# Per-head RMS means from split squares, and normed queries and keys placed by transfers, in a hybrid decoder layer

## The reference, cut to what matters

```python
def rmsnorm(x, g):
    x32 = x.astype(jnp.float32)
    y = x32 * lax.rsqrt(jnp.mean(x32 * x32, axis=-1, keepdims=True) + NORM_EPS)
    return (y * g.astype(jnp.float32)).astype(x.dtype)

q = rmsnorm(split_heads(q, NSA_HEADS), q_g)            # and the same for ks, kw, fox_q, fox_k
```

```python
a = jnp.exp(log_a)
b = jnp.sqrt(-jnp.expm1(2.0 * log_a)) * (i * xc).astype(jnp.float32)
_, h = lax.associative_scan(linear_combine, (a, b), axis=1)
return h.astype(u.dtype) * jax.nn.silu(z)
```

## Time and profile before

| what | value |
|---|---|
| median of 3 timed runs | 424.03 us (423.52 to 424.44) |
| the profiled execution | 423.8 us, its span 422.0 us |
| TensorE busy | 413.8 us, 98% of the span |
| VectorE busy | 286.5 us, 68% |
| ScalarE busy | 260.2 us, 62% |
| granted TensorE clock | 1.00 throughout |

### The profile page before, as it was taken

How to read it: one execution, slowest core, us unless ns; L and a number is a source line. 1 busy time by engine, 2 the same in 40 slices (tenths; PEclk the granted TensorE clock), 3 DMA queues, 4 the chain that set the end, 5 groups by cost and what they waited for, 6 DMA issues and landing times.

```text
span 422.0 us, 6560 instructions
## 1 busy us (share of the span) xinstructions
PE 413.8 (98%) x2234; PEld 325.8 (77%) x2234; DVE 286.5 (68%) x615; ACT 260.2 (62%) x516; POOL 65.6 (16%) x124
## 2 busy tenths in 40 slices
PE   8999999999999899999999999999899999999996
PEld 6876788879888766666677987988676688888885
DVE  3767749988998966776368756699877389422205
ACT  4846996687565887886087778771888554322200
POOL 5100000000000657565000000000466100000000
PEclk9999999999999999999999999999999999999999
DMA  7922534421213000000321323437610115721005
GB/s 265 355 82 96 161 95 125 120 73 45 101 50 102 0 1 2 2 1 2 119 90 66 101 75 119 132 96 181 189 42 2 50 57 208 279 96 61 2 0 199
DMA packets 13297, 40.51 MB, mean 96 GB/s; under 512 B 1848, under 2 KB 2104, under 8 KB 13008
## 3 DMA queue, kind: packets, MB, share of 16 engines
q1 hardware_dynamic: 13264, 40.09, 29.6%
HBM read 32.17 MB, written 2.10 MB: 81 GB/s over the span
## 4 chain that ended last, share of the span: by engine, by line
PE 84%; DVE 10%; issue 2%; ACT 1%; POOL 1%; POOLq 0%; DVEq 0%; ACTq 0%
PE bank L1417 12%; PE bank L1419 11%; PE bank L1418 11%; PE bank L1599 6%; PE bank L1580 6%; PE bank L1689 5%; PE bank L1688 5%; PE bank L1690 5%; PE bank L1570 4%; PE bank L1571 3%; PE bank L1489 2%; PE bank L1621 2%; PE bank L1390 2%; PE bank L1392 2%; PE bank L1391 2%
## 5 line engine op out<-in xcount | busy, mean ns | idle before, releaser
L1417 PE MATMUL bank<-xh,wh 128*128 128x512 f32 x240 | 99.7, 415 | 0.0
L1419 PE MATMUL bank<-xh,wl 128*128 128x512 f32 x240 | 93.8, 391 | 0.0
L1418 PE MATMUL bank<-xl,wh 128*128 128x512 f32 x240 | 93.8, 391 | 0.0
L997 DVE TENSOR_TENSOR wl<-raw,wh 128x1024 fp32r<-128x1024 f32 (+1 forms) x51 | 61.3, 1205 | 35.6 <-ACT wh L614 35.3
L614 ACT ACTIVATE wh<-raw 128x1024 fp32r<-128x1024 f32 (+1 forms) x51 | 52.6, 1038 | 30.9 <-PE bank L1690 28.4
L1417 PEld LDWEIGHTS bank<-xh,wh 128*128 128x128 f32 x240 | 45.1, 188 | 14.8 <-issue 5.4
L1221 DVE CUSTOM_DVE_ANT_0 bank<-bank,mask_row 128x256 f32<-128x256 f32 (+3 forms) x96 | 46.6, 499 | 13.1 <-PE bank L1571 12.8
L1418 PEld LDWEIGHTS bank<-xl,wh 128*128 128x128 f32 x240 | 45.2, 188 | 11.2 <-issue 2.6
L1419 PEld LDWEIGHTS bank<-xh,wl 128*128 128x128 f32 x240 | 45.1, 188 | 9.7
L591 POOL TENSOR_SCALAR probs<-probs,rcp,gates 128x384 f32<-128x384 f32 (+3 forms) x44 | 26.5, 613 | 136.3 <-DVE rcp L1241 136.2
L1688 PE MATMUL bank<-wh,yh 128*128 128x512 f32 x96 | 37.4, 389 | 0.0
(11 more groups left out here) (243 smaller groups left out, 769.7 us busy)
## 6 DMA issues: line engine op xcount, KB each, us to landing
raw<-in_w_in SPq DMA_DIRECT2D x36, 512.0 KB, 3.4
raw<-in_w_out SPq DMA_DIRECT2D x12, 512.0 KB, 3.3
x_raw<-in_xT SPq DMA_DIRECT2D x4, 512.0 KB, 7.5
x_res<-in_x_tok SPq DMA_DIRECT2D x1, 2048.0 KB, 9.6
out_y<-y_out SPq DMA_DIRECT2D x8, 256.0 KB, 2.2
raw<-in_w_in SPq DMA_DIRECT2D x3, 384.0 KB, 3.1
cmp_w_sb<-in_cmp_w SPq DMA_DIRECT2D x1, 1024.0 KB, 6.8
kh_fox<-kh_fox SPq DMA_DIRECT2D x8, 128.0 KB, 2.3
```

The source lines that it names most:

```text
L997: dve.tensor_tensor(wl[:, c % HL, cols], raw[:, c % RAW, cols], wh[:, c % HL, cols].bitcast(F32), ALU.subtract).then_inc(wl_ready, 1)
L1417: pe.matmul(dst, hi, xh[:, k, :], start=(k == 0), stop=False)
L1418: pe.matmul(dst, hi, xl[:, k, :], start=False, stop=False)
L1419: mm = pe.matmul(dst, lo, xh[:, k, :], start=False, stop=(k == KT - 1))
```

## The change

What it does, for each normed chunk:

- ScalarE also rounds the square to a high part, and VectorE writes the low part of the square (`square_low`). The mean is then two fp32r products with the rounded matrix `block_r`, accumulated in one bank; it stands ahead of block k = 7. Two banks alternate.
- The seeds lose the Identity; VectorE computes the Newton step from the mean in the bank, with constants folded into the gains (two small instructions at the start of the program).
- High and low parts of the normed chunk are each written whole (128 partitions) to one buffer `parts`, and four SP transfers per chunk bring them to their places. The next chunk's high part waits for all of them.
- ScalarE's square now stands ahead of the weight split.
- The recurrence tail of block 2 moves from nq 2 and vn 0 to fq 0 and fq 1 on VectorE, its output product from zl 3 to fq 2. Within a tail the order of instructions is as it was. Buffers are laid out anew for it.

The diff, cut to its core:

```diff
-TAIL_AT = (AT["ks", 0], AT["kw", 0], AT["nq", 0], AT["nq", 1], AT["nq", 2], AT["vn", 0], AT["vf", 2], AT["vf", 2])
+TAIL_AT = (AT["ks", 0], AT["kw", 0], AT["nq", 0], AT["nq", 1], AT["fq", 0], AT["fq", 1], AT["vf", 2], AT["vf", 2])
 OUT_ORDER = (2, 1, 0, 3)
...
         fg = v_nsa[:, :, VN_W - FG_W:]
+        with ExitStack() as w:
+            parts_nsa = sb("parts_nsa", [P, 4, SEQ], F32R, w)
         o_nsa = sb("o_nsa", [P, HEADS // 2, SEQ])
+        block_r = sb("block_r", [P, P], F32R)
         k_cmp_parts = sb("k_cmp_parts", [P, KVH, 2, CMP_PAD], F32R)
...
                     probs = sb("probs", [P, P_RING - 2, SEQ], F32, w)
+                    with ExitStack() as p:
+                        parts_fox = sb("parts_fox", [P, 4, SEQ], F32R, p)
                     pT = sb("pT", [P, 2, 2, PT_W], F32, w)
...
                 q_fox = sb("q_fox", [P, HEADS, SEQ], F32R, m)
-                kh_fox = sb("kh_fox", [P, HEADS, SEQ], F32R, m)
-                kl_fox = sb("kl_fox", [P, HEADS, SEQ], F32R, m)
+                k_fox = sb("k_fox", [P, HEADS, 2, SEQ], F32R, m)
                 q_first = sb("q_first", [P, 2, SEQ], F32R, m)
...
+        def norm_bank(n):
+            return (NORM_W if n % 2 else MEAN)[:, :]
         def nth_normed(c):
...
-            return sum({"nq": 0, "fq": 0, "fk": 2}.get(CHUNKS[x][0], 4) for x in NORMED[:c])
+            return 4 * c
+        def norm_parts(c):
+            return parts_nsa if nth_normed(c) < NSA_NORMED else parts_fox
...
-                n = nth_normed(c)
-                sp.wait_ge(h_ready, 2 * n + 2)
-                sp.wait_ge(l_ready, n + 1)
+                kind, j = CHUNKS[c]
+                sp.wait_ge(l_ready, nth_normed(c) + 1)
+                if nth_normed(c) == NSA_NORMED:
+                    sp.wait_ge(s_ready, NSA_UNITS)
+                parts = norm_parts(c)
                 for s in range(2):
                     own, other = half_of(s), half_of(1 - s)
-                    planes = key_planes(c, s)
-                    for plane in planes[:1] if CHUNKS[c][0] == "fk" else planes:
-                        sp.dma_start(plane[other, :].bitcast(F32), plane[own, :].bitcast(F32)).then_inc(stacked, 16)
+                    if kind in ("nq", "fq"):
+                        q = (q_nsa if kind == "nq" else q_fox)[:, 2 * j + s, :]
+                        copies = ((q[own, :], parts[own, 2, :]), (q[other, :], parts[own, 3, :]))
+                    elif kind == "fk":
+                        k = k_fox[:, 2 * j + s, :, :]
+                        copies = ((k[own, :, :], parts[own, 2:4, :]), (k[other, 0, :], parts[own, 2, :]))
+                    else:
+                        k = k_nsa[:, s + (KVH if kind == "kw" else 0), :, :]
+                        copies = ((k[own, :, :], parts[own, 2:4, :]), (k[other, :, :], parts[own, 2:4, :]))
+                    for dst, src in copies:
+                        sp.dma_start(dst.bitcast(F32), src.bitcast(F32)).then_inc(stacked, 16)
...
-                sp.wait_ge(h_ready, 2 * nth_normed(AT["fq", i]) + 2)
                 if i == 0:
+                    sp.wait_ge(stacked, 16 * stack_copies(nth_normed(AT["fq", 1]) + 1))
                     sp.wait_ge(cmp_prod, 2)
-                elif i in Q_SLOT:
+                else:
+                    sp.wait_ge(stacked, 16 * stack_copies(len(NORMED)))
+                if i in Q_SLOT:
                     sp.wait_ge(fox_consts, 4)
                     sp.wait_ge(proj_done, proj_units(Q_SLOT[i] - HL + 1))
-                else:
+                elif i > 0:
                     sp.wait_ge(s_ready, NSA_UNITS + PAIR_UNITS)
...
                 k = c - STACK_LAG
-                if 0 <= k < N_IN and CHUNKS[k][0] in ("ks", "kw", "fk"):
+                if k == AT["fq", 2]:
+                    place_queries(0)
+                if k in NORMED:
                     stack(k)
-                if k == AT["fq", 0]:
-                    place_queries(0)
                 if k == AT["vf", 3]:
...
                     act.activation(sq[:, :], qr[:, n % 2, :], ACT.Square).then_inc(sq_ready, 1)
+                    act.wait_ge(sq_ready, n + 1)
+                    act.activation(norm_parts(c)[:, 0, :], sq[:, :], ACT.Copy).then_inc(sq_high, 1)
...
                         act.wait_ge(normed, n)
-                    rsqrt_seed(MEAN[:, :], 64.0 if eighth else 1.0, std[:, :], work[:, :],
-                               NORM_W[:, :]).then_inc(norm_seed, 1)
+                    link(act.activation(std[:, :], norm_bank(n), ACT.Ln, bias=eps64 if eighth else eps1,
+                                        scale=64.0 if eighth else 1.0))
+                    link(act.activation(std[:, :], std[:, :], ACT.Exp, scale=-0.5))
+                    act.activation(work[:, :], std[:, :], ACT.Square).then_inc(norm_seed, 1)
...
                     act.wait_ge(normed, n + 1)
-                    if kind == "fq" and j == 0:
-                        act.wait_ge(s_ready, NSA_UNITS)
-                    for s in range(2):
-                        high, _ = operand_parts(c, s)
-                        act.activation(high, qr[half_of(s), n % 2, :], ACT.Copy).then_inc(h_ready, 1)
+                    if n >= 1:
+                        act.wait_ge(stacked, 16 * stack_copies(n))
+                    act.activation(norm_parts(c)[:, 2, :], qr[:, n % 2, :], ACT.Copy).then_inc(h_ready, 1)
...
                     dve.wait_ge(norm_seed, n + 1)
-                    link(dve.tensor_tensor(work[:, :], work[:, :], NORM_W[:, :], ALU.mult))
-                    link(dve.scalar_tensor_tensor(std[:, :], work[:, :], 1.5, std[:, :], ALU.add, ALU.mult))
+                    scale = 64.0 if kind in ("nq", "fq") else 1.0
+                    link(dve.scalar_tensor_tensor(work[:, :], norm_bank(n), EPS, work[:, :], ALU.add, ALU.mult))
+                    link(dve.scalar_tensor_tensor(std[:, :], work[:, :], -3.0 / scale, std[:, :], ALU.add, ALU.mult))
                     dve.scalar_tensor_tensor(qr[:, n % 2, :], qr[:, n % 2, :], ch(GAIN[kind]), std[:, :], ALU.mult,
...
                     n = nth_normed(c)
-                    for s in range(2):
-                        high, low = operand_parts(c, s)
-                        dve.wait_ge(h_ready, 2 * n + s + 1)
-                        ins = dve.tensor_tensor(low, qr[half_of(s), n % 2, :], high.bitcast(F32), ALU.subtract)
-                    ins.then_inc(l_ready, 1)
+                    parts = norm_parts(c)
+                    dve.wait_ge(h_ready, n + 1)
+                    dve.tensor_tensor(parts[:, 3, :], qr[:, n % 2, :], parts[:, 2, :].bitcast(F32),
+                                      ALU.subtract).then_inc(l_ready, 1)
+            def square_low(c):
+                if c in NORMED:
+                    parts = norm_parts(c)
+                    dve.wait_ge(sq_high, nth_normed(c) + 1)
+                    dve.tensor_tensor(parts[:, 1, :], sq[:, :], parts[:, 0, :].bitcast(F32),
+                                      ALU.subtract).then_inc(sq_low, 1)
...
                     zl_gate(2)
-                    lru_output(2)
                 evac(AT["zl", t])
...
                         gates_of(2)
-                    if k == KT // 2 + 1 and c - 1 in NORMED:
+                    if k == KT - 1 and c - 1 in NORMED:
                         head_mean(c - 1)
...
                 n = nth_normed(c)
-                pe.wait_ge(sq_ready, n + 1)
-                if n >= 1:
-                    pe.wait_ge(norm_seed, n)
-                pe.matmul(MEAN[:, :], block_mean, sq[:, :], start=True, stop=True).then_inc(norm_mean, 1)
+                pe.wait_ge(sq_low, n + 1)
+                if n >= 2:
+                    pe.wait_ge(normed, n - 1)
+                parts = norm_parts(c)
+                pe.matmul(norm_bank(n), block_r[:, :], parts[:, 0, :], start=True, stop=False)
+                pe.matmul(norm_bank(n), block_r[:, :], parts[:, 1, :], start=False, stop=True).then_inc(norm_mean, 1)
...
                     continue
+                if c in NORMED:
+                    before(c)
                 split_ahead(c)
                 if c == AT["u", 2]:
                     lru_sigmoids(0)
-                before(c)
+                if c not in NORMED:
+                    before(c)
...
                 norm(c - 1)
+                square_low(c)
                 low_parts(c - 1)
...
                 lru_tails(c)
+                if c == AT["fq", 2]:
+                    lru_output(2)
```

51 lines of the change are left out of this document (22 added, 29 removed).

## The result

The changed kernel takes 427.62 us (median of 4 runs, 426.90 to 429.23) beside 424.01 for the kernel before on the same chip (4 runs). The ratio is 1.0098, interval [1.0085, 1.0111]: one per cent slower, outside the forecast range. The four runs stand apart by TensorE's granted clock: 426.90 and 427.01 at a mean of 1.0, 428.22 at 0.996, 429.23 at 0.992. So 427.0 is the time at full clock, 3.0 us above the kernel before, and 0.7 of the 3.6 goes with the clock. The profiled one is the 426.90, span 425.1, and all rows of after are its.

The account below looks back on a forecast made before the run. TensorE, 98% busy, bounds the kernel, with VectorE's queue also full in the first stage. Of 5.6 us saved, 1.1 kept there, -0.2 compressed scores, -1.0 fox: 0.1 lost, giving 424.0 us, 8-in-10 range 421.2 to 426.0.

Parts of the forecast that it names:

- TensorE's part: Head means: one fp32 product of 0.86 us becomes two of 0.455 together, saving 0.40 us, 14 times: 5.6 us.
- The transfers: Four copies per normed chunk hold the parts buffer 4.2 us, mostly hidden; 0.2 us taken, at most 1 us.
- the compressed scores: Third k of zl0: they wait for nq3's copies, landed about 107.7, due 107.8; 0.2 us taken.
- a sign of being wrong: Forecast is wrong if its TensorE waits are absent, or if ScalarE's roundings wait for the copies.
- The slow rival: Copies become a loop: some 8 chunks in nq, fq, fk held 0.65 us each, 426.3 us; chance 0.23, including longer VectorE backlog.
- What the products wait for: Means wait for VectorE's low square: 1.35 us at vf 0 and vf 2, 1.5 fq 2, 0.6 nq0, 0.3 nq3.
- the addition: First stage: VectorE's queue added piece by piece from 61.75, putting nq0's low square at 75.8 and vn's start at 92.8.
- Fox stage: fq and fk: 8 means give 3.2 us back, waits cost 4.2, so 1.0 us lost.
- First stage: ks to nq3: vn starts at 92.8; 1.1 us of the stage's 2.4 us saving kept in all.
- The price of the tail: lru_tail(2, 1) behind fq 0's low parts on VectorE: a wait of 1.5 us at fq 2, caught up at fq 3.

Follow-up runs that it names:

- Experiment 8: Changed kernel with ks and kw high and low parts written in place by halves and stacked by two copies each: 425.80 us, ratio 1.0049.
- experiment 3: Changed kernel with the fp32 head mean at k = 5, no rounding or low part of the square; buffer, copies and tails kept: 424.23 us, ratio 1.0012.
- experiment 14: Changed kernel with the fp32 mean at k = 5, parts in place by halves, no square rounding or low square; tail stays in fox: 426.49 us, ratio 1.0068.
- kernel 6: Changed kernel with two parts buffers, lru_tail(2) at vn 0, low square ahead of the norm in three steps: 422.63 us, ratio 0.9981.
- Kernel 11: Changed kernel with parts in place by halves, two stacking copies for keys, and no low square (means not the reference's): 429.32 us, ratio 1.0141.
- kernel 10: Changed kernel without the low part of the square, both products reading the high part (means not the reference's): 425.85 us, ratio 1.0050.
- 9: kernel 6 with the first compressed scores at k = 5 of zl 0 and first transposes at k = 6 of zl 1: 423.44 us, ratio 0.9994.

## Why the prediction was wrong

**TensorE's part: right.** 0.40 us saved per mean was forecast; by the starts it is 0.86 - 0.47 = 0.39. (The records of the old product take 595 ns, not 591; the sum doesn't use them.)

**The transfers: this step failed.** The prediction said of the hold "1.9 + 2.3 = 4.2 us until the parts buffer is free", and of ks and kw that their copies "may take somewhat longer, but have a tail and a compression in their way". The four copies of ks, 256 KB each, took 3.2 us to issue and landed after 4.2 (median): a hold of 7.0. I had the landing from the key copies before, by halves of one plane, which are half the size, and the issue times from the same rows. ScalarE waited 1.60 and 2.96 us, VectorE 0.33 and 2.10 behind it. The sum had put this term at nothing but the 0.2 for the compressed scores, though the prediction named ScalarE's roundings waiting for the copies as a sign of being wrong. The sign is there.

The second buffer puts the kernel at +0.9 us against the forecast +0.1. The miss of 3.5 us against the forecast is thus 2.0 for the holds at full clock, 0.7 for the clock of the changed kernel's own runs, and 0.8 that stays (by the plain medians the buffer takes off 3.3, nearly all of it).

The slow rival had this mechanism, with a chance of 0.23, and the waits fell partly where it put them: 6.2 of ScalarE's 10.8 us are in nq, fq and fk. The hold in nq was near the forecast (low part of nq 1 ended at 93.90, next rounding at 98.17, 4.3 us), and ScalarE waited for it all the same, 1.43 us, because that low part was late, behind the second hold; for fq 2 it was 6.1. Its larger part is where it saw none, at ks and kw. It came to 426.3, closer than the forecast, with eight holds of 0.65 each, which isn't what happened. That was luck in the number. Experiment 8 shows that the holds of ks and kw alone cost 0.7 us net of the VectorE work that it adds. And experiment 3 shows that the same holds cost nothing with the old mean, which the forecast didn't ask: the price of a hold is set by what comes behind it.

**What the products wait for: right in kind, half right in size.** fq 2: 1.36 against 1.5. nq 0: 0.41 against 0.6. vf 0 and vf 2: 0.65 and 0.63 against 1.35 each. nq 3: 0.16 against 0.3. Not forecast at all: 1.56 at nq 2's mean, a product of the second hold. Up to the second hold the addition was right: nq 0's low square was ready at 75.58, forecast 75.8. The halved vf waits also come with something I had left out: the projections of vf themselves start late, by waits for wl of 0.37 and 0.51 us. The queue's delay is split between two of its results.

**Fox stage.** I called it 1.0 us lost. In after the stretch from fq 1's projection (207.93) to zn 0 (278.39) is 70.46 long, before it was 206.71 to 275.47, 68.76: 1.7 lost. The five waits there are 3.5 us by their records, less than the 4.2 forecast; with the 0.27 that each costs beyond its record they are 4.9, and 4.9 - 3.2 is 1.7. The copies of fq 2 hold ScalarE for 1.86 us at 238.90, those of fk for 1.47 and 0.75 later.

**First stage.** I said that vn would start at 92.8 and 1.1 us be kept. It started at 94.82 in after, at 93.06 with two buffers: the addition was right to 0.3 us but for the hold.

**The price of the tail: about right.** I gave its move a wait of 1.5 us at fq 2 and said that it "has caught up" at fq 3. Moving it away gave 2.2 us by the medians and 1.4 by the runs at full clock. By experiment 14 it, or ScalarE's order, costs 2.9 under the old mean too, with half-height low parts.

**The compressed scores** took 0.2 in the forecast; nothing of it shows in after, since the stage was late already. It came up at 1.43 in kernel 6, where TensorE gets there earlier: the estimate of a wait holds only for one arrival time.

What stays open is the price of the new mean itself. Kernel 11 has 5.6 us less for TensorE than kernel 14 and is 3.1 us slower; kernel 10 against 3, with copies, is 1.6 us slower (0.8 at full clock). Between the two of each pair are ScalarE's rounding of the square, the two products in place of one, and the mean's place at k = 7, two blocks later than before. All four runs of 11 were at a clock of 0.996 or less and all of 14 at 1.0, so part of the 3.1 goes with the clock. No run moves the split mean to an earlier block, so its place is an untested rival to everything that is put down to VectorE's queue. And of kernel 6's gain in the first stage little reaches the attention, since the scores wait (they start at 108.82, before the change at 108.94); 9 shows one chain behind them and not what is behind that.

## What to carry to other kernels

When an engine's saving rests on operands from another engine's queue, follow that queue in its order, with what it waits for itself, and not only its busy time: here VectorE was busy for 284.5 us instead of 286.5 and its results came late all the same. The single buffer, the low square and the tail's place cost 1.1 to 3.7 us each at full clock, and taking one away partly changed the name of TensorE's wait. A buffer that leaves by DMA is held from the first issue to the last landing, so take issue and landing times from transfers of the same size, and try a second one early: here it was worth 1.8 to 3.2 us at full clock. Compare medians only after the clocks of their runs. And measure a step alone and with its neighbours: the copies and the moved tail with the old mean cost 0.5 us, the whole change 4.2.
